# Gated units for two tiles in one slot, with products on 256 columns

## The chip, the cores and the metric

The kernel runs on one core of a Trainium2 chip, as one launch. The metric is the device time of that launch in microseconds. All values are float32.

## What is computed

The reference runs two layers of a trunk over a context of 128 tokens and a latent of 512 tokens, width 1024. Layer 0 is attention beside an RWKV mixer, layer 1 a convolution module, and each layer ends with an expert retrieval (`peer`). What matters here is layer 1's convolution module and the retrieval of both layers:

```python
def mixer_odd(h, w_pw1, b_pw1, w_dw, b_dw, ln_g, ln_b, w_pw2, b_pw2):
    u = h @ w_pw1 + b_pw1                               # 1024 -> 2048
    u = u[..., :D_CONV] * jax.nn.sigmoid(u[..., D_CONV:])
    u = depthwise_conv(u, w_dw) + b_dw                  # width 31
    u = jax.nn.silu(layernorm(u, ln_g, ln_b, LN_EPS))
    return u @ w_pw2 + b_pw2

def peer(h, w_q, keys, u_tab, v_tab):                   # per token: 8 heads, 16 experts each
    ...
        act = jax.nn.gelu(jnp.einsum('thkd,td->thk', u_tab[eidx], xb), approximate=False)
        wgt = (g * act.astype(jnp.float32)).astype(xb.dtype)
        return jnp.einsum('thk,thkd->td', wgt, v_tab[eidx])
```

Each token has 8 x 16 = 128 experts a layer, and an expert has a row of 1024 values in `u_tab` and one in `v_tab`.

## The kernel before

Up to some 900 us the kernel does layer 0's mixer. The rest, which the change touches, is `phase_trunk`. The 640 tokens are five tiles of 128: tile 0 is the context, tiles 1 to 4 the latent. Five tiles in two layers of `peer` make ten jobs, and a job has its own slot `s` of 128 rows (the loop over `PICKS`). In row `r` of slot `s`:

- GpSimd gathers, with an indirect DMA, one expert's `u` and `v` row for each of 128 tokens (128 x 2048 values) into one of `R = 8` places of `ring` (L1554). It waits until TensorE has used the place's earlier content (`used`).
- VectorE multiplies the `u` half with the tile's `h` and sums (`dot`, L1680), and does one step of choosing the experts of the next heads (`select`).
- ScalarE does, for two rows at a time, gelu, gate and the two scaled half identities `dg` (`weigh`, L1829 to L1840).
- TensorE adds the weighted `v` halves of two rows into PSUM with eight products on 512 columns (L2160 to L2164). I call these two rows a pair.

All other work of `phase_trunk` is laid beside these rows by hand. A generator such as `gated_units` yields the row number at which its next piece may be put, `Side` holds it, and `run_sides(sides, r)` writes out, on each engine, all pieces that are due by row `r` (TensorE and ScalarE look every second row). The row numbers thus set the order of instructions on an engine, not a time; semaphores do the rest. SyncE has no rows of its own: it goes through its pieces in the same order and stops at each wait.

Layer 1's convolution module of tile `i` has three parts, each with its slot:

- `GLU_SLOT(i)`, slots 2 to 6: the norm (`norm_one`: rows 12 to 21, scratch `y`, the two modulation rows in `pair`, and TensorE's transposes into `hT1`), then eight blocks of gated units, one each 4 rows from row 24. A block takes two weights of 128 x 1024 in `wg`, loaded by `for_glu` on SyncE's queue (L1500); TensorE does eight products each on the 128 columns of `hT1` (`units`, L2058), the second half two rows later; ScalarE does the sigmoid into `sg` (L1876), VectorE adds the bias, multiplies and writes `glu` (L1722). Each of the two `wg` places is loaded again once its product is done (`wg_used`).
- `CONV_SLOT(i)`, slots 2, 4, 5, 6, 7: the 31 taps from row 58 on. Five of eight blocks of channels are done on TensorE with scaled identities from ScalarE (`diagonals`, L1887; `taps`, L2076), three on VectorE. They need the units of the tile and of both neighbours, which is why tile 1's taps wait for tile 2's units.
- `POST_SLOT(i)`, slots 3, 5, 6, 7, 8: layer norm over channels (rows 4 to 18), the second linear layer (L2099, weights in `wq`, L1508), the gate and the sum (`mix`, rows 41 to 43), the second norm (`norm_two`, rows 46 to 50) and the queries and scores for the expert choice (L2126, weights in `wq`, L1480). `load_pair` (L1486, L1487) brings the two rows of 1024 values for each of norm, mix and second norm into the one `pair`, spread over all partitions (512 KB each); each load waits until the last user is done.

So slots 3, 5 and 6 hold units of one tile and the post part of another, slots 2 and 4 units alone, slots 7 and 8 the post part alone. On SyncE, `for_glu` and `for_post` write into one queue.

## Time and profile before

| | us |
|---|---|
| median of 3 runs | 4683.55 |
| lowest, highest | 4677.9, 4689.87 |
| the profiled execution | 4694.33 |
| its span, first to last instruction | 4692.5 |
| span's start to the end of slot 0 | 1408.6 |
| slots 1 to 9 | 3261.5 |
| TensorE, VectorE, ScalarE, GpSimd busy | 3236.1, 2775.4, 1728.1, 1468.9 |

The profile gives busy time for each engine; of the DMA it gives the share of time that the core's 16 DMA engines were busy (a little over 1 is possible, since packets overlap) and the GB/s that they moved. A slot is read as the time between two copies of `crossed` on ScalarE (L1848), which end a slot; the first of the ten starts at 1408.6 us, the last at 4670.1. "PEclk" is the granted clock of TensorE as a share of 2.4 GHz.

### The profile page before, as it was taken

To read this page: it belongs to the slowest core of one execution; us is meant where nothing else is said; L and a number is where in the kernel's file an instruction comes from. 1 tells how busy PE (TensorE), PEld (TensorE's weight loads), DVE (VectorE), ACT (ScalarE), POOL (GpSimd) and SP (SyncE) were. 2 spreads that over 40 slices of the span, in tenths; PEclk is the share of its full clock that TensorE was granted. 3 is DMA by queue.
4 is the path that set the end of the run, shared out by engine and by line. 5 is a ranking of instruction groups with operands and counts; after the bars stand their busy time and mean duration, and the time that the engine had idled before them with its cause. 6 is when DMAs were issued, how large, how long until landed. Compare 5 with 4: busy or idle time off the path is not lost. (4 is left out here: it accounts for less than half of the span.)

```text
span 4692.5 us, 72376 instructions
## 1 busy us (share of the span) xinstructions
PE 3236.1 (69%) x27071; PEld 1615.7 (34%) x27071; DVE 2775.4 (59%) x7104; ACT 1728.1 (37%) x5320; POOL 1468.9 (31%) x1298
## 2 busy tenths in 40 slices
PE   7988787777755556666665775786677677666555
PEld 4533676443211113323332332452344244223111
DVE  1257544335556766765656776585576776665764
ACT  1036222023222324544323553463454354332332
POOL 0000000012334443443334343343344443433443
PEclk9996898888877778988888887897898898888777
DMA  5161001268899999999999999999999999999998
GB/s 215 52 259 47 18 4 48 90 220 331 335 363 406 421 420 413 419 413 375 385 419 416 419 418 385 379 419 419 378 385 420 417 419 417 413 419 418 412 420 334
DMA packets 241982, 1567.70 MB, mean 334 GB/s; under 512 B 29942, under 2 KB 31057, under 8 KB 71265
## 3 DMA queue, kind: packets, MB, share of 16 engines
q0 software_dynamic: 184768, 1342.45, 69.8%
q1 hardware_dynamic: 56424, 220.51, 12.2%
q8 instruction: 216, 3.54, 0.3%
q14 instruction: 132, 1.08, 0.1%
q10 hardware_dynamic: 442, 0.12, 0.0%
HBM read 1559.88 MB, written 3.10 MB: 333 GB/s over the span
## 5 line engine op out<-in xcount | busy, mean ns | idle before, releaser
L1554 POOL DMA_INDIRECT t_ring<-in_peer_uv,t_eidx x1280 | 1461.4, 1142 | 3181.7 <-PE t_ps L2164 2051.3
L2160 PE MATMUL t_ps<-t_ring,t_dg 64*64 64x512 f32 x2560 | 1584.0, 751 | 1145.4 <-ACT t_dg L1840 1107.5
L1680 DVE SCALAR_TENSOR_TENSOR t_ring<-t_ring,t_hring 128x1024 f32<-128x1024 f32 x1024 | 1253.6, 1224 | 841.5 <-DMA t_ring<-in_peer_uv,t_eidx 810.3
L2164 PE MATMUL t_ps<-t_ring,t_dg 64*64 64x512 f32 x2560 | 1601.7, 758 | 0.0
L2163 PE MATMUL t_ps<-t_ring,t_dg 64*64 64x512 f32 x2560 | 1601.4, 758 | 0.0
L2161 PE MATMUL t_ps<-t_ring,t_dg 64*64 64x512 f32 x2560 | 1601.0, 758 | 0.0
L2160 PEld LDWEIGHTS t_ps<-t_ring,t_dg 64*64 64x64 f32 x2560 | 347.9, 157 | 2093.3 <-issue 2063.7
L1829 ACT ACTIVATE t_wgt<-t_dots 128x2 f32<-128x2 f32 x640 | 130.2, 203 | 1872.9 <-DVE t_ring L1680 1824.4
L1680 DVE SCALAR_TENSOR_TENSOR t_ring<-t_ring,t_early 128x1024 f32<-128x1024 f32 x256 | 313.8, 1226 | 313.8 <-DMA t_ring<-in_peer_uv,t_eidx 312.3
L1840 ACT ACTIVATE t_dg<-t_eye,t_wgt 128x64 f32<-128x64 f32 x1280 | 376.8, 340 | 2.7 <-ACT t_wgt L1834 1.9
L2164 PEld LDWEIGHTS t_ps<-t_ring,t_dg 64*64 64x64 f32 x2560 | 349.0, 157 | 0.0
L2163 PEld LDWEIGHTS t_ps<-t_ring,t_dg 64*64 64x64 f32 x2560 | 348.8, 157 | 0.0
L2161 PEld LDWEIGHTS t_ps<-t_ring,t_dg 64*64 64x64 f32 x2560 | 348.7, 157 | 0.0
L1834 ACT ACTIVATE t_wgt<-t_wgt,t_gate 128x1 f32<-128x1 f32 x1280 | 307.1, 287 | 26.1 <-ACT t_wgt L1829 0.4
L1887 ACT ACTIVATE t_early<-ident,vec 128x128 f32<-128x128 f32 x775 | 236.5, 389 | 0.7
L2058 PE MATMUL t_ps<-t_hT,t_wg 128*128 128x128 f32 x1280 | 180.6, 299 | 72.4 <-DMA t_wg<-in_cv_w_pw 72.4
L2076 PEld LDWEIGHTS t_ps<-t_early 128*128 128x128 f32 x1550 | 189.2, 195 | 74.7 <-ACT t_early L1887 43.2
L2058 PEld LDWEIGHTS t_ps<-t_hT,t_wg 128*128 128x128 f32 x1280 | 165.0, 209 | 144.6 <-issue 121.0
L2076 PE MATMUL t_ps<-t_early 128*128 128x128 f32 x1550 | 207.3, 287 | 5.4 <-PE t_ps L2126 0.5
L318 PE MATMUL fr_ps<-ev_hT,ev_wring 128*128 128x512 f32 x336 | 174.3, 601 | 0.0
L2126 PE MATMUL t_ps<-t_hT,t_wq 128*128 128x128 f32 x1280 | 162.3, 282 | 0.0
L2126 PEld LDWEIGHTS t_ps<-t_hT,t_wq 128*128 128x128 f32 x1280 | 156.4, 199 | 4.9 <-issue 4.9
(367 smaller groups left out, 4465.3 us busy)
## 6 DMA issues: line engine op xcount, KB each, us to landing
t_wq<-in_peer_w_q SPq DMA_DIRECT2D x112, 512.0 KB
ev_mod_ring<-in_mod_w SPq DMA_DIRECT2D x48, 1024.0 KB, 10.0
t_wg<-in_cv_w_pw SPq DMA_DIRECT2D x80, 512.0 KB
t_ring<-in_peer_uv,t_eidx POOLq DMA_INDIRECT x1280
t_wq<-in_cv_w_pw SPq DMA_DIRECT2D x40, 512.0 KB
t_pair<-modrows SPq DMA_DIRECT2D x25, 512.0 KB
ev_wring<-in_ab_w_in SPq DMA_DIRECT2D x21, 512.0 KB, 3.6
ev_qk<-in_ab_w_out SPq DMA_DIRECT2D x1, 4096.0 KB, 12.1
```

The source lines that it names most:

```text
L1554: pool.indirect_dma_start(ring[:, place[n], :], None, table, bass.IndirectOffsetOnAxis(ap=eidx[:, s % 2, r:r + 1], axis=0)).then_inc(row_i ...
L1680: V.scalar_tensor_tensor(ring[:, place[n], 0:D], ring[:, place[n], 0:D], 1.0, h_of(j), ALU.mult, ALU.mult, accum_out=dots[:, j % 2, r:r + ...
L1834: nc.scalar.activation(wgt[:, r + b:r + b + 1], wgt[:, r + b:r + b + 1], ACT.Copy, scale=gate[:, j % 2, r + b:r + b + 1]).then_inc(S["wgt_ ...
L1840: nc.scalar.activation(dg[:, n % DIAGS, :], eye[:], ACT.Copy, scale=wgt[:, r + b:r + b + 1]).then_inc(S["diag_set"], 1)
L1887: nc.scalar.activation(diag[:, n % BATCH, :], ident[:], ACT.Copy, scale=K.vec[:, col:col + 1]).then_inc(S["diag_ready"], 1)
L2058: last = nc.tensor.matmul(banks[:, 4 + b % 2, a * P:(a + 1) * P], wg[:, a, k, :], hT1[:, k, :], start=(k == 0), stop=(k == KD - 1))
L2076: nc.tensor.matmul(banks[:, 4 + b % 2, 0:P], diag[:, n % BATCH, :], glu[:, b, glu_col(i) + w:glu_col(i) + w + P], start=(w == 0), stop=(w ...
L2126: last = nc.tensor.matmul(banks[:, 6 + b % 2, 0:P], wq[:, n % 2, k, :], hT1[:, k, :], start=(k == 0), stop=(k == KD - 1))
L2160: nc.tensor.matmul(straight[low, cols], dg[low, n % DIAGS, :], ring[low, one, rows], **ends)
L2161: first = nc.tensor.matmul(straight[high, cols], dg[high, n % DIAGS, :], ring[high, one, rows], **ends)
L2163: nc.tensor.matmul(crossed[high, cols], dg[low, (n + 1) % DIAGS, :], ring[low, two, rows], **ends)
L2164: second = nc.tensor.matmul(crossed[low, cols], dg[high, (n + 1) % DIAGS, :], ring[high, two, rows], **ends)
```

## The change

The tiles' gated units are grouped: tiles 0 and 1 in slot 2, tiles 2 and 3 in slot 4, tile 4 alone in slot 6. In a group of two, both normed tiles are transposed (the first with rows from 4 on, the second from 12 on) into two halves of a buffer `both`, and each weight is used for one product on 256 columns. Such a block comes every 6 rows from row 22; tile 4's come every 4 rows, from row 22 as well. The sigmoid is one instruction for both tiles, with one buffer instead of two (ScalarE looks every second row, so `+ 3` and `+ 4` are the same place), and VectorE does two products of 128 columns in a block. Tile 3's norm uses the modulation rows that tile 2's has loaded. `CONV_SLOT` and `POST_SLOT` stay; in slots 2 and 4 taps and diagonals start at row 72, not 58. `cv`, `diag` and `hT1` get other places inside `early`, so that `both` can lie over `cv` and `hT1`.

```diff
-    GLU_SLOT = lambda i: i + 2
+    GROUPS = ((0, 1), (2, 3), (4,))
+    group = lambda i: i // 2
+    GLU_SLOT = lambda i: 2 + 2 * group(i)
...
+    glu_tick = lambda g, b: 22 + (6 if len(GROUPS[g]) == 2 else 4) * b
+    conv_tick = lambda i: 72 if CONV_SLOT(i) in (2, 4) else 58
+    glu_base = lambda i: 4 if i in (0, 2) else 12
...
+    units_in = lambda i: KD * (1 + (group(min(i + 1, NT - 1)) if i else 0))
...
-        early = sb("early", [P, 8672])
+        early = sb("early", [P, 9696])
...
-        cv = early[:, 5600:6624].rearrange("p (k c) -> p k c", k=KD)
+        cv = early[:, 7648:8672].rearrange("p (k c) -> p k c", k=KD)
+        both = early[:, 7648:9696].rearrange("p (t k c) -> p k t c", t=2, k=KD)
...
-        diag = early[:, 7648:7648 + BATCH * P].rearrange("p (n c) -> p n c", c=P)
-        hT1 = sb("hT1", [P, KD, P])
+        diag = early[:, 5600:5600 + BATCH * P].rearrange("p (n c) -> p n c", c=P)
+        hT1 = early[:, 8672:9696].rearrange("p (k c) -> p k c", k=KD)
...
-                def for_glu(i):
-                    yield 2
-                    load_pair(("norm", i), mod_row(i, 1), mod_row(i, 0))
+                def for_glu(g):
+                    for i in GROUPS[g]:
+                        yield glu_base(i) - 4
+                        if i != 3:
+                            load_pair(("norm", i), mod_row(i, 1), mod_row(i, 0))
                     for b in range(KD):
-                        yield 18 + 4 * b
+                        yield glu_tick(g, b) - 6
                         for a in range(2):
-                            n = 2 * (KD * i + b) + a
+                            n = 2 * (KD * g + b) + a
                             if n >= 2:
                                 sp.wait_ge(S["wg_used"], n - 1)
                             sp.dma_start(wg[:, a].rearrange("p k c -> p (k c)"), io["cv_w_pw1"][0, a * KD + b]).then_inc(wg_in[a], 16)
...
                 def norm_one(i):
-                    yield 14
+                    yield glu_base(i) + 2
                     mean(NORMS["norm", i])
-                    yield 16
+                    yield glu_base(i) + 4
                     invert(NORMS["norm", i])
                     dve.wait_ge(S["pair_in"], 32 * (PAIRS["norm", i] + 1))
+                    if i:
+                        dve.wait_ge(S["turned1"], i)
                     m = own(V.scalar_tensor_tensor(y, x[:, i, :], rstd[:, NORMS["norm", i]:NORMS["norm", i] + 1], pair[:, 0, :], ALU.mult, ALU.mult))
-                    yield 18
+                    yield glu_base(i) + 6
                     after_own(m)
                     V.tensor_tensor(y, y, pair[:, 1, :], ALU.add).then_inc(S["h1_done"], 1)
                     dve.wait_ge(S["h1_done"], i + 1)
-                    dve.sem_inc(S["pair_used"], 1)
-
...
-                def gated_units(i):
-                    col = glu_col(i) + PADC
+                    if i != 2:
+                        dve.sem_inc(S["pair_used"], 1)
+
+                def gated_units(g):
                     for b in range(KD):
-                        yield 24 + 4 * b + 6
-                        n = KD * i + b
+                        yield glu_tick(g, b) + 6
+                        n = KD * g + b
                         dve.wait_ge(S["sig_done"], n + 1)
                         bias = VEC["cv_b_pw1"] + b
-                        V.scalar_tensor_tensor(glu[:, b, col:col + P], banks[:, 4 + b % 2, 0:P], K.vec[:, bias:bias + 1], sg[:, b % 2, :],
-                                               ALU.add, ALU.mult).then_inc(S["glu_done"], 1)
+                        for e, i in enumerate(GROUPS[g]):
+                            col = glu_col(i) + PADC
+                            last = V.scalar_tensor_tensor(glu[:, b, col:col + P], banks[:, 4 + b % 2, e * P:(e + 1) * P], K.vec[:, bias:bias + 1], sg[:, e, :],
+                                                          ALU.add, ALU.mult)
+                        last.then_inc(S["glu_done"], 1)
...
-                    yield 61
+                    yield conv_tick(i) + 3
                     if i == 0:
                         dve.wait_ge(S["padded"], 4)
                     else:
                         dve.wait_ge(S["w_done"], i)
-                    dve.wait_ge(S["glu_done"], KD * min(i + 2 if i else 1, NT))
+                    dve.wait_ge(S["glu_done"], units_in(i))
...
                 def norm_one(i):
-                    yield 12
+                    yield glu_base(i)
                     act.wait_ge(S["summed"], GLU_SLOT(i))
-                    act.wait_ge(S["var_done"], done_by(POST_SLOT, GLU_SLOT(i)))
-                    square(y, i, NORMS["norm", i])
-                    yield 15
+                    act.wait_ge(S["q_done"], Q0 + NC * done_by(POST_SLOT, GLU_SLOT(i) - 1))
+                    dst = turned_tile(i)
+                    square(dst, i, NORMS["norm", i])
+                    yield glu_base(i) + 3
                     root(NORMS["norm", i])
-                    yield 21
+                    yield glu_base(i) + 9
                     act.wait_ge(S["turned1"], i + 1)
-                    act.wait_ge(S["q_done"], Q0 + NC * done_by(POST_SLOT, GLU_SLOT(i) - 1))
-                    nc.scalar.copy(hT1[:].rearrange("p k t -> p (k t)"), ps[:, 2, :]).then_inc(S["hTa_done"], 1)
-
-                def sigmoids(i):
+                    nc.scalar.copy(dst, ps[:, 2, :]).then_inc(S["hTa_done"], 1)
+
+                def sigmoids(g):
                     for b in range(KD):
-                        yield 24 + 4 * b + 3
-                        n = KD * i + b
+                        yield glu_tick(g, b) + 4
+                        n, members = KD * g + b, len(GROUPS[g])
                         act.wait_ge(S["g_done"], n + 1)
-                        if n >= 2:
-                            act.wait_ge(S["glu_done"], n - 1)
+                        if n:
+                            act.wait_ge(S["glu_done"], n)
                         bias = VEC["cv_b_pw1"] + KD + b
-                        nc.scalar.activation(sg[:, b % 2, :], banks[:, 4 + b % 2, P:2 * P], ACT.Sigmoid, bias=K.vec[:, bias:bias + 1]).then_inc(S["sig_done"], 1)
+                        nc.scalar.activation(sg[:, 0:members, :], banks[:, 4 + b % 2, 2 * P:(2 + members) * P].rearrange("p (t c) -> p t c", c=P),
+                                             ACT.Sigmoid, bias=K.vec[:, bias:bias + 1]).then_inc(S["sig_done"], 1)
...
                 def norm_one(i):
-                    yield 20
+                    yield glu_base(i) + 8
                     pe.wait_ge(S["h1_done"], i + 1)
                     if done_by(CONV_SLOT, GLU_SLOT(i) - 1):
                         pe.wait_ge(S["block_out"], NPE * done_by(CONV_SLOT, GLU_SLOT(i) - 1))
+                    if glu_base(i) > 4 and i < NT - 1:
+                        pe.wait_ge(S["hTa_done"], i)
                     for k in range(KD):
                         last = nc.tensor.transpose(ps[:, 2, k * P:(k + 1) * P], y[:, k * P:(k + 1) * P], ident[:])
                     last.then_inc(S["turned1"], 1)
 
-                def units(i):
+                def units(g):
+                    members = GROUPS[g]
+                    N = len(members) * P
                     for b in range(KD):
-                        yield 24 + 4 * b
-                        n = KD * i + b
+                        yield glu_tick(g, b)
+                        n = KD * g + b
                         if b == 0:
-                            pe.wait_ge(S["hTa_done"], i + 1)
+                            pe.wait_ge(S["hTa_done"], members[-1] + 1)
                         if n >= 2:
                             pe.wait_ge(S["glu_done"], n - 1)
                         for a in range(2):
                             if a:
-                                yield 26 + 4 * b
+                                yield glu_tick(g, b) + 2
                             pe.wait_ge(wg_in[a], 16 * (n + 1))
                             for k in range(KD):
-                                last = nc.tensor.matmul(banks[:, 4 + b % 2, a * P:(a + 1) * P], wg[:, a, k, :], hT1[:, k, :], start=(k == 0), stop=(k == KD - 1))
+                                rhs = both[:, k, :, :] if len(members) == 2 else hT1[:, k, :]
+                                last = nc.tensor.matmul(banks[:, 4 + b % 2, 2 * a * P:2 * a * P + N], wg[:, a, k, :], rhs, start=(k == 0), stop=(k == KD - 1))
```

The same shift of rows (`conv_tick(i)` for 58, `conv_tick(i) + 3` for 61) is made in `diagonals`, `blocks` and TensorE's `taps`. Lines of `phase_trunk` move by up to 27: L2058 is L2084 in the changed kernel, L2099 is L2125, L2160 is L2187, L1500 is L1513, L1508 is L1521, L1722 is L1739.

On SyncE, from the norm of slot 2 to the post part of slot 3. `t_pair` are modulation rows, `t_wg` the units' weights, `t_wq` from `in_cv_w_pw` the second linear layer's. Before:

```order
L1486 DMA t_pair<-modrows 128x1024
L1487 DMA t_pair<-modrows 128x1024
L1500 DMA t_wg<-in_cv_w_pw 128x1024 x16
L1486 DMA t_pair<-modrows 128x1024
L1487 DMA t_pair<-modrows 128x1024
L1508 DMA t_wq<-in_cv_w_pw 128x1024
L1500 DMA t_wg<-in_cv_w_pw 128x1024 x2
L1508 DMA t_wq<-in_cv_w_pw 128x1024 x2
L1486 DMA t_pair<-modrows 128x1024
L1487 DMA t_pair<-in_cv_b_pw 128x1024
L1500 DMA t_wg<-in_cv_w_pw 128x1024 x2
L1508 DMA t_wq<-in_cv_w_pw 128x1024 x2
```

and with the change:

```order
L1497 DMA t_pair<-modrows 128x1024
L1498 DMA t_pair<-modrows 128x1024
L1497 DMA t_pair<-modrows 128x1024
L1498 DMA t_pair<-modrows 128x1024
L1513 DMA t_wg<-in_cv_w_pw 128x1024 x16
L1521 DMA t_wq<-in_cv_w_pw 128x1024 x3
L1497 DMA t_pair<-modrows 128x1024
L1498 DMA t_pair<-in_cv_b_pw 128x1024
L1521 DMA t_wq<-in_cv_w_pw 128x1024 x5
L1497 DMA t_pair<-modrows 128x1024
L1498 DMA t_pair<-modrows 128x1024
L1491 DMA t_wq<-in_peer_w_q 128x1024 x16
```

Slot 3 has no `t_wg` any more, and slot 2 has two loads of rows ahead of its sixteen weights. On SyncE again, the start of slot 6. Before:

```order
L1486 DMA t_pair<-modrows 128x1024
L1487 DMA t_pair<-modrows 128x1024
L1521 DMA t_grow<-modrows 128x1024
L1508 DMA t_wq<-in_cv_w_pw 128x1024
L1500 DMA t_wg<-in_cv_w_pw 128x1024 x2
L1508 DMA t_wq<-in_cv_w_pw 128x1024 x2
L1486 DMA t_pair<-modrows 128x1024
L1487 DMA t_pair<-in_cv_b_pw 128x1024
L1500 DMA t_wg<-in_cv_w_pw 128x1024 x2
L1508 DMA t_wq<-in_cv_w_pw 128x1024 x2
L1500 DMA t_wg<-in_cv_w_pw 128x1024 x2
L1508 DMA t_wq<-in_cv_w_pw 128x1024 x2
```

and with the change:

```order
L1497 DMA t_pair<-modrows 128x1024
L1498 DMA t_pair<-modrows 128x1024
L1534 DMA t_grow<-modrows 128x1024
L1513 DMA t_wg<-in_cv_w_pw 128x1024 x2
L1521 DMA t_wq<-in_cv_w_pw 128x1024 x2
L1513 DMA t_wg<-in_cv_w_pw 128x1024 x2
L1521 DMA t_wq<-in_cv_w_pw 128x1024
L1497 DMA t_pair<-modrows 128x1024
L1498 DMA t_pair<-in_cv_b_pw 128x1024
L1521 DMA t_wq<-in_cv_w_pw 128x1024
L1513 DMA t_wg<-in_cv_w_pw 128x1024 x2
L1521 DMA t_wq<-in_cv_w_pw 128x1024 x2
```

The weights of units come two rows earlier against those of the post part: two `t_wg` blocks now stand ahead of the `t_pair` row from `in_cv_b_pw`. On TensorE, in slot 2, from the first half of a block of units to the second. Before:

```order
L2058 MATMUL t_ps<-t_hT,t_wg 128x128 x8
L2160 MATMUL t_ps<-t_ring,t_dg 64x512
L2161 MATMUL t_ps<-t_ring,t_dg 64x512
L2163 MATMUL t_ps<-t_ring,t_dg 64x512
L2164 MATMUL t_ps<-t_ring,t_dg 64x512
L2160 MATMUL t_ps<-t_ring,t_dg 64x512
L2161 MATMUL t_ps<-t_ring,t_dg 64x512
L2163 MATMUL t_ps<-t_ring,t_dg 64x512
L2164 MATMUL t_ps<-t_ring,t_dg 64x512
L2058 MATMUL t_ps<-t_hT,t_wg 128x128 x8
```

and with the change:

```order
L2084 MATMUL t_ps<-t_early,t_wg 128x256 x8
L2187 MATMUL t_ps<-t_ring,t_dg 64x512
L2188 MATMUL t_ps<-t_ring,t_dg 64x512
L2190 MATMUL t_ps<-t_ring,t_dg 64x512
L2191 MATMUL t_ps<-t_ring,t_dg 64x512
L2187 MATMUL t_ps<-t_ring,t_dg 64x512
L2188 MATMUL t_ps<-t_ring,t_dg 64x512
L2190 MATMUL t_ps<-t_ring,t_dg 64x512
L2191 MATMUL t_ps<-t_ring,t_dg 64x512
L2084 MATMUL t_ps<-t_early,t_wg 128x256 x8
```

Between the two halves of a block stands one pair, as before; each product has 256 columns. Behind the second half stood one pair up to the next block, now there are two.

## Rows read from the trace of the kernel before

**Rows 1.** The page: DMA by 40 equal slices of the span, and queue q0
```profile
DMA  5161001268899999999999999999999999999998
GB/s 215 52 259 47 18 4 48 90 220 331 335 363 406 421 420 413 419 413 375 385 419 416 419 418 385 379 419 419 378 385 420 417 419 417 413 419 418 412 420 334
...
q0 software_dynamic: 184768, 1342.45, 69.8%
```

**Rows 2.** Windows, one for each of slots 1 to 8; columns as printed
```profile
core 0: us, PE busy (x) PEld busy (x) DVE busy (x) ACT busy (x) POOL busy (x), PEclk, DMA share, GB/s
1408.60:1744.50 335.90, 190.86 (x1032) 49.51 (x1032) 221.12 (x572) 98.71 (x346) 149.28 (x132) 0.74 1.01 417
1744.50:2093.50 349.00, 231.71 (x1606) 115.64 (x1606) 247.56 (x679) 170.86 (x533) 145.11 (x128) 0.88 1.01 417
2093.50:2489.80 396.30, 253.90 (x1656) 127.46 (x1656) 230.64 (x589) 141.74 (x424) 147.86 (x128) 0.85 0.97 395
2489.80:2835.00 345.20, 231.63 (x1606) 113.71 (x1606) 248.40 (x679) 171.12 (x533) 144.87 (x128) 0.88 1.01 418
2835.00:3233.80 398.80, 286.60 (x1966) 159.09 (x1966) 255.28 (x685) 188.49 (x584) 147.98 (x128) 0.86 0.98 397
3233.80:3633.20 399.40, 281.30 (x1966) 156.91 (x1966) 254.13 (x685) 188.10 (x583) 152.46 (x128) 0.88 0.97 397
3633.20:3991.40 358.20, 253.99 (x1702) 125.43 (x1702) 251.50 (x672) 164.21 (x556) 148.92 (x128) 0.88 1.01 418
3991.40:4349.20 357.80, 221.14 (x1392) 90.09 (x1392) 230.52 (x585) 117.33 (x397) 141.07 (x128) 0.87 1.01 417
```

**Rows 3.** Waits (in total, times, longest): slot 2, slot 3's start, slot 6's start
```profile
POOL t_ring L1554 <- PE t_ps L2164: 183.1, 62, 6.9
...
POOL t_ring L1554 <- PE t_ps L2164: 126.0, 28, 20.7
...
DVE t_hring L1781 <- DMA t_pair<-modrows: 13.7, 1, 13.7
```

**Rows 4.** Windows, 40 us of slot 3
```profile
2260.00:2300.00 40.00, 24.89 (x172) 13.72 (x176) 29.45 (x77) 16.86 (x45) 15.73 (x12) 0.78 0.80 322
```

**Rows 5.** Timelines of SyncE, TensorE and VectorE in slot 3 (start, us, what, [idle before])
```profile
2164.80 2.77 SPq L1500 DMA_DIRECT2D t_wg<-in_cv_w_pw  x2
...
2183.84 3.75 PE L2058 MATMUL t_ps<-t_hT,t_wg 128*128 128x128 f32 x16 [12.50 <-DMA t_wg<-in_cv_w_pw]
...
2247.49 0.43 SPq L1486 DMA_DIRECT2D t_pair<-modrows  x1
...
2262.60 1.29 DVE L1781 SCALAR_TENSOR_TENSOR t_hring<-x,t_rstd,t_pair 128x1024 f32<-128x1024 f32 x1 [12.57 <-DMA t_pair<-modrows]
```

**Rows 6.** The page: DMA issues, with count and KB each
```profile
t_wg<-in_cv_w_pw SPq DMA_DIRECT2D x80, 512.0 KB
```

**Rows 7.** Timeline of TensorE in slot 3: a block of units, a product on 512 columns
```profile
2165.16 2.05 PE L2058 MATMUL t_ps<-t_hT,t_wg 128*128 128x128 f32 x16
...
2219.28 2.01 PE L2099 MATMUL t_ps<-t_wq,t_early 128*128 128x512 f32 x4
```

**Rows 8.** Timeline of TensorE: first and last instruction of two pairs of sixteen
```profile
2097.85 0.64 PE L2160 MATMUL t_ps<-t_ring,t_dg 64*64 64x512 f32 x1 [1.33 <-DVE t_early L1691]
...
2099.21 0.59 PE L2164 MATMUL t_ps<-t_ring,t_dg 64*64 64x512 f32 x1
...
2143.35 1.08 PE L2160 MATMUL t_ps<-t_ring,t_dg 64*64 64x512 f32 x1 [5.30 <-ACT t_dg L1840]
...
2145.98 1.06 PE L2164 MATMUL t_ps<-t_ring,t_dg 64*64 64x512 f32 x1
```

**Rows 9.** Windows: slot 2 up to 1860 us and behind it, 40 us of slot 5
```profile
1744.50:1860.00 115.50, 77.73 (x499) 36.67 (x500) 80.44 (x224) 49.32 (x132) 43.54 (x42) 0.82 1.01 413
1860.00:1940.00 80.00, 49.51 (x368) 28.39 (x366) 52.14 (x148) 40.56 (x114) 32.16 (x26) 0.94 1.02 418
2940.00:2980.00 40.00, 34.20 (x208) 18.83 (x206) 18.83 (x50) 14.91 (x35) 12.19 (x12) 0.91 0.98 393
```

**Rows 10.** Groups of ScalarE: table loads at the sigmoid's line (count, busy, mean ns)
```profile
L1876 ACT ACT_TABLE_LOAD x40 | 51.3, 1283 | 0.7
```

More of the change, by code:

```diff
@@ L1458, in phase_trunk @@
             for i in range(NT):
-                if GLU_SLOT(i) == s:
+                if GLU_SLOT(i) == s and i != 3:
                     PAIRS["norm", i] = len(PAIRS)
@@ L1465, in phase_trunk @@
         at_slot = lambda of, s: [i for i in range(NT) if of(i) == s]
+        groups_at = lambda s: [g for g in range(len(GROUPS)) if GLU_SLOT(GROUPS[g][0]) == s]
+        last_group = lambda s: sum(GLU_SLOT(members[0]) <= s for members in GROUPS)
+        PAIRS["norm", 3] = PAIRS["norm", 2]
         NORMS = {}
@@ L1537, in _ @@
                         sides.append(Side(next_keys()))
-                    sides += [Side(for_glu(i)) for i in at_slot(GLU_SLOT, s)]
+                    sides += [Side(for_glu(g)) for g in groups_at(s)]
                     sides += [Side(for_post(i)) for i in at_slot(POST_SLOT, s)]
@@ L1761, in mix @@
                     dve.wait_ge(S["pair_in"], 32 * (PAIRS["mix", i] + 1))
-                    if POST_SLOT(i) in [GLU_SLOT(k) for k in range(NT)]:
-                        dve.wait_ge(S["turned1"], POST_SLOT(i) - 1)
+                    if at_slot(GLU_SLOT, POST_SLOT(i)):
+                        dve.wait_ge(S["turned1"], done_by(GLU_SLOT, POST_SLOT(i)))
                     m = own(V.tensor_tensor(y, ps[:, 3, :], pair[:, 1, :], ALU.add))
@@ L1974, in _ @@
                     for i in at_slot(GLU_SLOT, s):
-                        sides += [Side(norm_one(i)), Side(sigmoids(i))]
+                        sides.append(Side(norm_one(i)))
+                    sides += [Side(sigmoids(g)) for g in groups_at(s)]
                     for i in at_slot(POST_SLOT, s):
@@ L2069, in taps @@
                         if m == 0:
-                            pe.wait_ge(S["glu_done"], KD * min(i + 2 if i else 1, NT))
+                            pe.wait_ge(S["glu_done"], units_in(i))
                             if i == 0:
@@ L2141, in _ @@
                     for i in at_slot(GLU_SLOT, s):
-                        sides += [Side(norm_one(i)), Side(units(i))]
+                        sides.append(Side(norm_one(i)))
+                    sides += [Side(units(g)) for g in groups_at(s)]
                     for i in at_slot(POST_SLOT, s):
```

16 lines of the change are left out of this document (9 added, 7 removed).

## The prediction

> **What bounds the kernel now.** I read the page's 40 slices first. From the 13th slice on (a slice is 117.3 us long, so from about 1408 us) the DMA digit is 9 and GB/s lies between 375 and 421, up to the last slice [rows 1]. No compute engine is near that: TensorE is busy for 69% of the span. In this part the kernel works through ten jobs, and each job fetches 128 times a block of 128 expert rows. That is 1280 gathers that carry 1342.45 MB, or 1.049 MB each [rows 1]. Per job, the windows [rows 2] show two kinds. Slots 2, 4, 7 and 8 run at 417 to 418 GB/s with a DMA share of 1.01; slots 3, 5 and 6 take 396.3, 398.8 and 399.4 us at 395 to 397 GB/s with a share of 0.97 to 0.98. So in the first kind the end is set by bytes, and in the second by bytes plus holes.
>
> The waits by window tell what the holes are. In slot 2, GpSimd (which issues gathers) never waits over 6.9 us for TensorE to free a ring place. In the first half of slot 3 it waits up to 20.7 us [rows 3], and the DMA share falls as low as 0.80 over 40 us [rows 4]. TensorE itself is held there: 12.50 us for a weight block of the gated units, which was issued at 2164.80, in SyncE's order right behind two `t_wq` blocks and two `t_pair` rows. VectorE waits 12.57 us for the `t_pair` rows issued at 2247.49 [rows 5]. Slots 3, 5 and 6 are those in which gated units (`for_glu`) and the second half of a convolution (`for_post`) share SyncE's one queue, where each load can stand behind another one's wait.
>
> **Bytes that go.** Each of eight blocks per tile loads two `t_wg` weights of 512 KB: 80 loads now [rows 6]. With three groups instead of five tiles there are 48. The `t_pair` rows of tile 3's norm go too (2 loads), since tile 2's are kept. That is 34 loads of 0.524 MB; at 417 GB/s [rows 2] one is 1.257 us of all engines, so 42.7 us in sum. The Trainium skill, "DMA: Bandwidth & Descriptors", section "Bandwidth", says that between HBM and SBUF the HBM side binds at about 358 GB/s for a core; by that the 34 loads would be an estimated 49.8 us. The trace does not agree: it has 417 to 418 GB/s over whole slots [rows 2].
>
> **Bytes and holes, slot by slot.** Instead of adding a price of holes to this, I take for each slot the slot of before that has the same work.
> - Slot 3 keeps the post part alone. So does slot 8 now: 357.8 us. 396.3 - 357.8 = 38.5 us less.
> - Slot 5 keeps post and taps, as slot 7 has now: 358.2 us, plus one `t_grow` load (1.3 us) that slot 7 lacks: 359.5. 398.8 - 359.5 = 39.3 us less.
> - Slot 2 gets the `t_pair` rows of tile 1 beside those of tile 0: 2 x 1.257 = 2.5 us more.
> - Slot 4 has 16 weight loads and one pair of rows before and after: 0.
> The sum is 38.5 + 39.3 - 2.5 = 75.3 us. Of this, 42.7 are bytes and the other 32.6 are holes and small traffic.
>
> **What the doubled products cost.** A block of 8 products on 128 columns (16 matmul instructions) took 2.05 us at the higher clock and 3.75 us where the clock was low [rows 5]; 4 instructions on 512 columns took 2.01 us, 0.50 each, so 256 columns are 0.25 each [rows 7]. Sixteen of those are 4.0 us, and twice the 128-column block is 4.1 us (7.5 at the low clock, by the 3.75 us block of [rows 5]). So grouping saves no TensorE time; it puts 31 us more (16 x 1.95) into slot 2 and into slot 4, off the path as long as TensorE keeps up. The order shows what it has to keep up with: in rows 22 to 70 of the slot, six picks a block. Gathers and loads need 6 x 2.51 + 2 x 1.257 = 17.6 us a block. TensorE needs three pairs, at 1.95 us (2097.85 to 2099.80) or 3.7 us (2143.35 to 2147.04) [rows 8], and two blocks of 4.1 or 7.5: 14.1 us at 2.4 GHz, 26.1 us at 1.2 GHz. The granted clock was 0.82 in the stretch with the units of slot 2, then 0.94 [rows 9]; at 0.95 the block is about 14.8 us, 84% of 17.6. The nearest row with as dense a TensorE is that of the 40 us from 2940: 34.20 us busy, 86%, with a DMA share of 0.98 where 1.01 is full [rows 9]. That is 3% lost. Over 8 x 17.6 = 141 us it is 4 us a slot, 8 us in both. The ends: 0 (the ring of 8 places takes it all), or what slot 3 lost. There 32.6 us of holes in two slots say 16 us for one, so 32 for two. I take 8, because the 12 to 13 us waits of slot 3 came from SyncE's queue, and in slots 2 and 4 that queue holds nothing but `t_wg` in these rows.
>
> **Slot 6** keeps gated units, post and taps together. The units start 2 rows earlier, and the order of SyncE's queue changes: the weights of the second block now stand ahead of the third `t_wq` and of the bias rows, which they followed before, and the last `t_pair` rows no longer wait for TensorE's row 46 but for its row 44. Two rows are 5 us of the 13.7 us that VectorE waited for such rows in slot 6 [rows 3]. I take 5 us off; the ends are 16 (its hole closes) and -3 (the sigmoid, now with one buffer, holds VectorE once a block for a little).
>
> **Taps 14 rows later.** In slots 2 and 4 taps run in rows 72 to 126, not 58 to 112. The same instructions at the same spacing; over the whole of slot 2 TensorE was busy for 231.71 of 349.0 us and VectorE for 247.56 [rows 2], so they stay hidden. The mean over channels at row 4 of the next slot reads what row 126 finishes: the cover shrinks from 20 rows to 6, 15 us. If it were gone, each of two slots would show one wait of a few us; I count 0, up to 5. On ScalarE each sigmoid costs a table load of 1.28 us and one back for Gelu [rows 10]; 16 fewer of each free 41 us there. It waits for VectorE most of the time, so that is worth 0. The second norm in slots 2 and 4 (two VectorE operations of 1.2 us, a copy of 1.0 on ScalarE, eight transposes) is hidden by the same slack: 0.
>
> **Waits that it adds.** VectorE's second norm (row 16) waits for TensorE's transposes of the first tile (row 12), and the dots of row 16 and on stand behind it; four rows, 10 us, cover it. On SyncE the second `t_pair` load of slot 2 waits for VectorE's row 10, with sixteen `t_wg` behind it; the first of these is needed at row 22, some 30 us on, and rows issued at 2247.49 had landed by 2262.60 [rows 5]. TensorE's second transposes (row 20) wait for ScalarE's copy (row 14), with the pair of rows 20 and 21 behind. The sigmoid of a block waits until VectorE has used the one before, with ScalarE's gelu behind it, and VectorE has two rows, 5 us, for that. Each is counted at 0; one that shows would cost at most a wait of 7 us as slot 2 has now on GpSimd's side [rows 3], and the ring of eight took those without a hole.
>
> **Sum.** -75.3 + 8 - 5 = -72.3 us. The profiled execution took 4694.33 us (span 4692.5), 10.8 us over the median of the runs, 4683.55; the difference is carried over to the median: 4683.55 - 72.3 = 4611 us.
>
> **The rivals.**
> 1. *The holes move.* TensorE's bursts hold the ring in slots 2 and 4 as slots 3 and 5 are held now: 16 us each in place of 4. For it: 84% is as dense as any stretch of now, and the single buffer for the sigmoid ties VectorE, ScalarE and TensorE once a block. Against: in rows 22 to 70 nothing else stands in SyncE's queue. Time: 4683.55 - 75.3 - 5 + 32 = 4635 us.
> 2. *No loss at all.* Slots 2 and 4 lose nothing, slot 6 closes: 4683.55 - 75.3 - 16 = 4592 us.
> 3. *Slower: TensorE bounds rows 22 to 70 at the low clock.* At 1.2 GHz a block needs 26.1 us against 17.6, 8.5 us more; 16 blocks are 136 us, and with the 75.3 and the 5 us gained 4739 us. It decides from 5.0 us a block on (80.3 / 16), so from a block of 22.6 us, a clock that stays low for most of it. Against: the clock rose as the stretch went on, from 0.82 to 0.94 [rows 9].
> 4. *It doesn't pay.* The slots without holes are set by something that counts gathers, not bytes, and the holes come back: within 14 us of 4684. Against: slot 1, nearly without loads, took 335.9 us, slots 7 and 8, with 28, took 358 [rows 2].
>
> **Chances.** Forecast (4597 to 4628) 0.68; rival 1 0.18; rival 2 0.06; rival 3 0.04; rival 4 0.04. The range must leave out no more than 0.2: from 4595 to 4642 it holds the forecast and nearly all of rival 1. A measurement of this kernel tells about 0.3%, 14 us, from no change. The forecast and rivals 1 and 2 are all faster by more than that: faster 0.92, same 0.04, slower 0.04.
>
> **What will show it.** Loads: `t_wg` x48 and 17.8 MB less in all. Slot 3 near 358 us and slot 5 near 360 at 417 GB/s, with no wait of GpSimd over 10 us: right; if they stay above 370, the holes were not of the shared queue. Slot 2 near 355 and slot 4 near 349: right; 365 and more is rival 1, above all with a DMA share under 0.95 in rows 22 to 70; a granted clock near 0.5 there is rival 3. Slot 6 near 394. The forecast would be wrong if the 256-column products were much dearer than 0.25 us an instruction.

## The result, and the profile after

| | us |
|---|---|
| changed kernel, median of 4 runs | 4598.51 (4595.88 to 4602.11) |
| kernel before, beside it | 4680.73 (4677.72 to 4689.87) |
| ratio, 95% interval | 0.9822 [0.9805, 0.9839] |
| its profiled execution, span | 4601.10, 4599.3 |

The change took 82 us off, 1.8%, where 72 were forecast. The time lies in the forecast range of 4597 to 4628, near its low end, 12.5 us under the 4611 forecast.

The windows of the changed kernel, slots 1 to 8, between two copies of `crossed` (L1867 there), with the columns of [rows 2]:

```profile
core 0: us, PE busy (x) PEld busy (x) DVE busy (x) ACT busy (x) POOL busy (x), PEclk, DMA share, GB/s
1405.00:1737.80 332.80, 188.62 (x1032) 49.28 (x1032) 220.72 (x572) 98.70 (x345) 146.32 (x132) 0.75 1.01 417
1737.80:2085.30 347.50, 251.68 (x1614) 130.65 (x1614) 250.32 (x686) 177.61 (x540) 145.11 (x128) 0.91 1.01 416
2085.30:2446.50 361.20, 231.75 (x1392) 96.90 (x1392) 228.84 (x582) 117.74 (x396) 142.71 (x128) 0.83 1.01 417
2446.50:2789.90 343.40, 251.99 (x1614) 131.02 (x1614) 253.15 (x691) 177.92 (x540) 144.14 (x128) 0.91 1.01 414
2789.90:3153.30 363.40, 254.50 (x1702) 125.86 (x1702) 251.76 (x675) 163.97 (x557) 152.48 (x128) 0.89 1.01 416
3153.30:3539.40 386.10, 280.46 (x1966) 157.22 (x1966) 253.70 (x682) 190.52 (x586) 143.34 (x128) 0.89 1.00 409
3539.40:3898.10 358.70, 257.67 (x1702) 126.88 (x1702) 251.33 (x672) 164.45 (x557) 143.54 (x128) 0.88 1.01 417
3898.10:4255.30 357.20, 220.80 (x1392) 91.05 (x1392) 229.80 (x585) 117.11 (x397) 140.90 (x128) 0.88 1.01 417
```

Against [rows 2], slots 3 and 5 have lost the share of 0.97 to 0.98 and stand at 1.01 with 361.2 and 363.4 us. Slots 2 and 4 carry twice the products (TensorE is busy for 20 us more in each, where 31 were forecast) at a full DMA share and a little less time. Slot 6 still has a hole, a smaller one. From these windows:

| slot | before | after | difference | forecast |
|---|---|---|---|---|
| 1 | 335.9 | 332.8 | -3.1 | 0 |
| 2 | 349.0 | 347.5 | -1.5 | +6.5 |
| 3 | 396.3 | 361.2 | -35.1 | -38.5 |
| 4 | 345.2 | 343.4 | -1.8 | +4 |
| 5 | 398.8 | 363.4 | -35.4 | -39.3 |
| 6 | 399.4 | 386.1 | -13.3 | -5 |
| 7 and 8 | 716.0 | 715.9 | -0.1 | 0 |

The list of DMA issues shows the loads that went, beside the 80 of [rows 6]; the last number is the median time from issue to landing:

```profile
t_wg<-in_cv_w_pw SPq DMA_DIRECT2D x48, 512.0 KB, 8.1
...
t_pair<-modrows SPq DMA_DIRECT2D x23, 512.0 KB, 11.6
...
t_pair<-in_cv_b_pw SPq DMA_DIRECT2D x5, 512.0 KB, 15.0
```

The packets sum up to 1549.80 MB against 1567.70 MB, 17.9 MB less. The waits of the changed kernel in the whole of slot 3 and in slot 6's first 207 us, in the form of [rows 3]:

```profile
POOL t_ring L1567 <- PE t_ps L2191: 198.7, 62, 6.4
...
POOL t_ring L1567 <- PE t_ps L2191: 128.1, 32, 16.1
...
PE t_ps L2084 <- DMA t_wg<-in_cv_w_pw: 16.8, 4, 11.3
...
DVE t_hring L1799 <- DMA t_pair<-modrows: 8.2, 1, 8.2
```

In slot 3 GpSimd now waits 6.4 us at most, where it was 20.7 [rows 3]. In slot 6, the one slot in which units and post part still meet, it is 16.1 us, and TensorE and VectorE wait for the same two kinds of load as before.

### The profile page after: what moved, and what is told of

Read it like the earlier page. It is cut to its first block and busy times, and to the rows that moved or that the text cites. A ratio compares the mean times of both kernels' runs of the same rounds, so it can differ in the third digit from the quotient of the medians.

```text
span 4599.3 us, 71228 instructions
## 1 busy us (share of the span) xinstructions
PE 3223.2 (70%) x26559; PEld 1588.6 (35%) x26559; DVE 2775.9 (60%) x7104; ACT 1695.2 (37%) x5282; POOL 1447.1 (31%) x1298
## 2 busy tenths in 40 slices
DMA packets 237081, 1549.80 MB, mean 337 GB/s; under 512 B 29398, under 2 KB 30513, under 8 KB 66369
## 5 line engine op out<-in xcount | busy, mean ns | idle before, releaser
L1567 POOL DMA_INDIRECT t_ring<-in_peer_uv,t_eidx x1280 | 1439.6, 1125 | 3110.3 <-PE t_ps L2191 1981.2
L2187 PE MATMUL t_ps<-t_ring,t_dg 64*64 64x512 f32 x2560 | 1578.4, 749 | 1124.7 <-ACT t_dg L1859 1102.5
L2187 PEld LDWEIGHTS t_ps<-t_ring,t_dg 64*64 64x64 f32 x2560 | 347.5, 156 | 2085.0 <-issue 2055.6
L2084 PE MATMUL t_ps<-t_early,t_wg 128*128 128x256 f32 (+1 forms) x768 | 157.0, 360 | 16.8 <-DMA t_wg<-in_cv_w_pw 16.8
L2152 PE MATMUL t_ps<-t_early,t_wq 128*128 128x128 f32 x1280 | 165.1, 285 | 0.0
L2152 PEld LDWEIGHTS t_ps<-t_early,t_wq 128*128 128x128 f32 x1280 | 159.6, 203 | 4.1 <-issue 4.1
L2084 PEld LDWEIGHTS t_ps<-t_early,t_wg 128*128 128x128 f32 x768 | 128.9, 198 | 74.6 <-issue 57.5
## 6 DMA issues: line engine op xcount, KB each, us to landing
t_ring<-in_peer_uv,t_eidx POOLq DMA_INDIRECT x1280, 13.3
```

Source lines behind the costliest of these rows:

```text
L1567: pool.indirect_dma_start(ring[:, place[n], :], None, table, bass.IndirectOffsetOnAxis(ap=eidx[:, s % 2, r:r + 1], axis=0)).then_inc(row_i ...
L2084: last = nc.tensor.matmul(banks[:, 4 + b % 2, 2 * a * P:2 * a * P + N], wg[:, a, k, :], rhs, start=(k == 0), stop=(k == KD - 1))
L2152: last = nc.tensor.matmul(banks[:, 6 + b % 2, 0:P], wq[:, n % 2, k, :], hT1[:, k, :], start=(k == 0), stop=(k == KD - 1))
L2187: nc.tensor.matmul(straight[low, cols], dg[low, n % DIAGS, :], ring[low, one, rows], **ends)
```

## The experiments

Two pictures of where the time came from had to be told apart. In mine, the end is set by bytes, and the holes (time in which less is moved than the 414 to 418 GB/s of a full slot) are waits behind other loads in SyncE's queue. In the other, the holes belong to the work itself (TensorE and VectorE in the rows where units and post part meet), or to any load beside it. Eleven runs follow; one of them is the changed kernel again, one a repeat. Ratios are against the kernel before, measured beside each, with 95% intervals; they and the medians can differ by some us in what they give, and where it matters both are told. Slot times are from one profile each: in six profiles with the same work in slots 3 and 5, slot 3 took 359.5 to 361.4 us and slot 5 361.8 to 364.9.

**Only the bytes put back.** In slots 3 and 5 of the changed kernel, where the weight places are idle, ScalarE makes 16 loads a slot into them that nobody uses:

```diff
+                def extra_loads(q):
+                    for b in range(KD):
+                        yield 24 + 6 * b
+                        if b == 0:
+                            act.wait_ge(S["wg_used"], 2 * KD * (q + 1))
+                        if b or q:
+                            act.wait_ge(S["extra_in"], 32 * (KD * q + b))
+                        for a in range(2):
+                            act.dma_start(wg[:, a]...).then_inc(S["extra_in"], 16)
...
+                            if b == 0 and a == 0 and g:
+                                sp.wait_ge(S["extra_in"], 32 * KD * g)
...
+                    if s in (3, 5):
+                        sides.append(Side(extra_loads((s - 3) // 2)))
```

The wait on SyncE holds the first real weight of slots 4 and 6 until the extra loads are in.

> The changed kernel with the 32 weight loads that the grouping removed put back as loads that nobody uses: 16 in slot 3 and 16 in slot 5, two every 6 rows, issued by ScalarE into the idle weight places, so not in SyncE's queue. Theory A (the end is set by bytes, and the holes came from the shared queue): slots 3 and 5 get 20 us longer each (361 to 381, 363 to 383), DMA share stays at 1.01, the whole is 40 us slower than the changed kernel (about 4639 us), still 42 us faster than before. Rival B (fewer, not smaller: the slots are set by a count of gathers): within 10 us of the changed kernel. Rival C (any 16 more loads beside the post part make the holes, whoever issues them): slots 3 and 5 return to 395 us or more, the whole to 4665 or more.

Measured: 4633.18 us, ratio 0.9897 [0.9877, 0.9917]. Slots 3 and 5 in its windows:

```profile
2088.60:2470.60 382.00, 236.40 (x1392) 96.62 (x1392) 229.83 (x584) 117.17 (x396) 142.91 (x128) 0.80 1.01 416
2812.00:3194.80 382.80, 261.20 (x1702) 127.14 (x1702) 251.59 (x673) 163.65 (x557) 143.56 (x128) 0.86 1.01 415
```

They are 20.8 and 19.4 us longer than in the changed kernel, 40.2 for 32 loads: 1.26 us a load, where 1.257 was worked out. With a scatter of one to three us a slot, the agreement to the last digit is chance. The whole is 35 us slower than the changed kernel, by the medians and by the ratios, or 1.1 us a load; 40 had been expected. The profiled execution was the slowest of four. The share stays at 1.01. So bytes are paid in full or nearly so, and 16 more loads beside the post part make no hole when they come from elsewhere.

What did the holes cost? The same two slots of the kernel before took 396.3 and 398.8 us [rows 2], 14.3 and 16.0 more than here. But slot 3 of before moved fewer bytes (395 GB/s in 396.3 us are 156.5 MB, against 158.9 here). Taken by the rate, 395 and 397 GB/s in place of 416, an estimated 20 and 18 us of those slots were hole. Between the two readings lie 30 to 38 us for both slots.

**Only the modulation rows moved, in the kernel before.**

```diff
-                        if k == 2:
-                            load_pair(("mix", i), mod_row(i, 2), io["cv_b_pw2"][0])
                     yield 43
-                    load_pair(("keys", i), mod_row(i, 4), mod_row(i, 3))
...
+                def pairs_of_post(i):
+                    row = lambda kind: K.modrows[stream(i), (6 + kind) * D:(7 + kind) * D]
+                    for tick, key, first, second in ((20, "mix", row(2), io["cv_b_pw2"][0]), (44, "keys", row(4), row(3))):
+                        yield tick
+                        act.wait_ge(S["pair_used"], PAIRS[key, i])
+                        act.dma_start(pair[:, 0, :], first.partition_broadcast(P)).then_inc(S["pair_in"], 16)
+                        act.dma_start(pair[:, 1, :], second.partition_broadcast(P)).then_inc(S["pair_in"], 16)
```

> The kernel before, with only one thing moved: the modulation rows of mix and of the second norm (the pair loads of the post part, 512 KB each) are issued by ScalarE at rows 20 and 44, not by SyncE between the weight loads. Theory A (holes of slots 3, 5 and 6 come from loads that stand behind another load's wait in the one queue): VectorE's wait of 12 to 14 us for these rows falls to 8 us or less in each, and TensorE's of 12.5 us for the second block's weight falls too; slots 3, 5, 6 get 5 to 12 us shorter each, the whole 15 to 35 us faster than before. Rival B (the holes come from the work of TensorE and VectorE in those rows, not from the queue): within 8 us of before.

Measured: 4644.22 us, ratio 0.9929 [0.9910, 0.9949]: 39 us by the medians, 33 by the ratio, at the upper end of what was expected or a little over it. The windows of slots 3, 5 and 6, and the waits in slot 3's first 210 us:

```profile
2080.20:2464.80 384.60, 257.38 (x1656) 127.00 (x1656) 231.53 (x593) 141.57 (x423) 143.77 (x128) 0.86 1.00 407
2809.00:3196.70 387.70, 285.65 (x1966) 157.31 (x1966) 256.13 (x689) 188.26 (x583) 146.22 (x128) 0.89 1.00 411
3196.70:3584.50 387.80, 289.09 (x1966) 160.65 (x1966) 255.26 (x687) 188.37 (x584) 146.03 (x128) 0.88 1.00 409
```

```profile
POOL t_ring L1551 <- PE t_ps L2169: 124.9, 33, 10.4
...
PE t_ps L2063 <- DMA t_wg<-in_cv_w_pw: 17.7, 7, 5.1
...
DVE t_hring L1778 <- DMA t_pair<-modrows: 1.4, 1, 1.4
```

Every slot with both kinds of work is 11 to 12 us shorter, with the same loads and products (slot 3 moved 156.5 MB in both, by its rates). TensorE's longest wait for a weight is 5.1 us where it was 12.50, VectorE's for the rows 1.4 for 12.57, GpSimd's longest 10.4 for 20.7. The two pictures part here: the work was left as it was, so it can't be the cause of the part that went; where and when the loads are issued is. The edit changes the issuing engine and the row of issue together, and no run parts these two. Nor is the hole gone. The three slots run at 407 to 411 GB/s, not 416, which makes an estimated 5 to 8 us of hole that is left in each, of some 18 to 20 before; TensorE's waits for weights in these 210 us still sum up to 17.7.

**Only the row of the units moved, in the kernel before.** All five tiles' units two rows earlier, as tile 4's are in the change:

```diff
-                        yield 18 + 4 * b
+                        yield 16 + 4 * b
...
-                        yield 24 + 4 * b
+                        yield 22 + 4 * b
```

(and the same two rows for the second half, the sigmoid and VectorE's product).

> The kernel before with one part of the change alone: all five tiles' blocks of units start at row 22 in place of 24, loads of their weights two rows earlier too; no grouping. Theory A (order and rows close most of the hole that units and post part make together): slots 3, 5 and 6 each get about 13 us shorter, the whole 35 to 40 us faster than before (about 4643 us), with no byte less. Rival B: no slot moves by over 4 us, the whole within 10 us of before.

Measured: 4661.59 us, ratio 0.9963 [0.9951, 0.9975]: 17 us by the ratio, 21 by the medians. Slots 3, 5 and 6:

```profile
2081.60:2470.10 388.50, 249.37 (x1656) 123.51 (x1656) 232.04 (x592) 144.22 (x425) 139.46 (x128) 0.87 0.99 403
2814.90:3207.30 392.40, 280.67 (x1966) 156.49 (x1966) 253.61 (x685) 190.96 (x586) 140.52 (x128) 0.89 0.99 403
3207.30:3600.70 393.40, 287.82 (x1966) 158.06 (x1966) 256.22 (x686) 191.13 (x586) 148.20 (x128) 0.87 1.00 406
```

That is 7.8, 6.4 and 6.0 us a slot, half of the 13 I had expected after seeing slot 6 of the changed kernel. The gain is there, at half the size.

**The same row, undone in the changed kernel.** Tile 4's units from row 24:

```diff
-    glu_tick = lambda g, b: 22 + (6 if len(GROUPS[g]) == 2 else 4) * b
+    glu_tick = lambda g, b: 22 + 6 * b if len(GROUPS[g]) == 2 else 24 + 4 * b
```

> The changed kernel with one part undone: tile 4's blocks of units start at row 24 again, not at row 22 (slot 6), so that SyncE's order in slot 6 is that of the kernel before. Theory A (slot 6 became 13.3 us shorter, 399.4 to 386.1, because the weights and modulation rows are asked for in another order and two rows earlier): slot 6 returns to 396 to 400 us and the whole is 10 to 14 us slower than the changed kernel (4609 to 4612 us). Rival B (it came from the single sigmoid buffer, the place of hT1, or chance): slot 6 stays at 384 to 388, the whole within 4 us of 4598.5.

Measured: 4602.94 us, ratio 0.9844 [0.9822, 0.9867]; slot 6 at 395.6. The slot came near to what theory A said; the whole is 4 us above the 4598.5 of the changed kernel, not 10 to 14. Slot 6 was also at 388.5, 390.1 and 393.2 us in three other kernels with the changed kernel's instructions in that slot, so one profile says little, and both kernels were measured again side by side.

> The changed kernel as it is, on the same chip and in the same rounds as the next one, which puts tile 4's units back to row 24: its slot 6 was 386.1 us in one profile, but 388.5, 390.1 and 393.2 in three kernels with the same instructions in that slot. Expected: 390 +- 4 us for slot 6, 4598 us for the whole.

> The changed kernel with tile 4's units at row 24. Theory A (order and rows are worth 6 us in slot 6, as in three slots of the kernel before): slot 6 at 395 to 397, the whole 4 to 8 us slower than the changed kernel of the same call. Rival B (they are worth nothing, and slot 6 only scatters): within 2 us of it.

Measured: 4595.13 us, ratio 0.9806 [0.9792, 0.9821], and 4600.94 us, ratio 0.9821 [0.9804, 0.9838]: 5.8 us between the medians, though the intervals overlap. Slot 6 of the one and of the other, and what VectorE waits for the modulation rows in each:

```profile
3141.50:3534.10 392.60, 285.47 (x1966) 158.69 (x1966) 256.50 (x686) 191.23 (x585) 146.39 (x128) 0.87 1.00 406
...
DVE t_hring L1799 <- DMA t_pair<-modrows: 9.1, 1, 9.1
```

```profile
3145.70:3540.60 394.90, 286.38 (x1966) 158.57 (x1966) 255.37 (x685) 188.26 (x583) 149.03 (x128) 0.87 0.98 401
...
DVE t_hring L1799 <- DMA t_pair<-modrows: 12.2, 1, 12.2
```

With the units at row 22 VectorE waits 8.2 and 9.1 us in two profiles, at row 24 13.2 and 12.2: with the gain goes this wait, 3 to 5 us shorter. Five profiles with row 22 have slot 6 at 386.1, 388.5, 390.1, 392.6 and 393.2 us, 390.1 in the mean; two with row 24 at 395.6 and 394.9; the kernel before, and before with later taps (below), at 399.4 and 398.5. So the row is worth about 5 us in slot 6. Some 4 us lie between 395 and 399; with two profiles on either side they may be something else in the change, the single sigmoid buffer or the new places in `early`, or scatter. No run tells which.

**Both small moves, in the kernel before.** Units at row 22 and the modulation rows from ScalarE (the two edits above).

> The kernel before with both small moves: units of all tiles at row 22, and the modulation rows of the post part issued by ScalarE; no grouping, no byte less. Theory A (the holes of slots 3, 5 and 6 are the waits behind other loads in SyncE's queue, and both moves take away some of the same): slots 3, 5, 6 at 382 to 385 us, which is what the same bytes took when they came from elsewhere, the whole 42 to 48 us faster than before (4635 to 4640 us); what is left to the changed kernel is the 42 us of bytes. Rival B (the moves add up, 17 and 39): 56 us faster.

Measured: 4645.02 us, ratio 0.9912 [0.9894, 0.9930]: 41 us by the ratio, 42 by the medians. By the ratios alone a sum of 17 and 33 us can't be told from this, since each of these has an interval of 11 to 18 us. The slots can tell. Slots 3, 5 and 6:

```profile
2078.40:2462.10 383.70, 262.76 (x1656) 129.03 (x1656) 232.51 (x592) 144.45 (x425) 143.81 (x128) 0.84 1.00 408
2805.50:3195.40 389.90, 285.33 (x1966) 158.09 (x1966) 257.30 (x689) 191.63 (x585) 150.80 (x128) 0.89 1.00 409
3195.40:3581.50 386.10, 287.64 (x1966) 159.88 (x1966) 255.61 (x686) 191.47 (x586) 150.28 (x128) 0.88 1.01 412
```

In sum they are 0.4 us shorter than with the modulation rows alone, where adding up would have made them 20 us shorter. So the moves take away the same hole; they don't add up. About half of the gain of the changed kernel is thus to be had without grouping anything.

**The width of the product.** The changed kernel with two runs of eight products on 128 columns for each weight:

```diff
-                            for k in range(KD):
-                                rhs = both[:, k, :, :] if len(members) == 2 else hT1[:, k, :]
...
+                            for e in range(len(members)):
+                                for k in range(KD):
+                                    rhs = both[:, k, e, :] if len(members) == 2 else hT1[:, k, :]
...
```

(each product then writes its own 128 columns).

> The changed kernel, but in slots 2 and 4 each weight is used for two runs of eight products on 128 columns in place of one run of eight on 256; loads, rows and groups stay. Theory A (the gain is that each weight is loaded once for two tiles; the width of the product is nothing, since TensorE has slack): 32 instructions of 0.128 us are 4.1 us for what took 3.72, slots 2 and 4 within 3 us of 347.5 and 343.4, the whole within 10 us of 4598.5. Rival B (256 columns are what keeps slots 2 and 4 full): each 8 us or more longer.

Measured: 4595.91 us, ratio 0.9816 [0.9796, 0.9835]. The blocks on TensorE, of this kernel and then of the changed one:

```profile
1813.59 3.84 PE L2085 MATMUL t_ps<-t_early,t_wg 128*128 128x128 f32 x32
```

```profile
1813.10 3.72 PE L2084 MATMUL t_ps<-t_early,t_wg 128*128 128x256 f32 x16
```

Slots 2 and 4 took 348.6 and 341.1 us. The width is worth nothing here; the weight that is loaded once is the gain.

**TensorE's slack.** Each run of eight products on 256 columns done twice:

```diff
-                            for k in range(KD):
+                            for k in [k for _ in members for k in range(KD)]:
```

> The changed kernel, but in slots 2 and 4 each run of eight products on 256 columns is done twice (7.4 us for 3.72), loads and rows as they are. A block of six rows has 17.6 us by bytes; TensorE then needs 3 x 1.95 + 4 x 3.72 = 20.7 us. Theory A (the block is set by the dearer of the two, and the slack now is 17.6 less 13.3 us): slots 2 and 4 get about 3 to 5 us a block longer, 25 to 40 us each, the whole 4648 to 4678 us. Rival B (the ring takes more, since other rows have slack): under 10 us each.

Measured: 4651.26 us, ratio 0.9932 [0.9912, 0.9952]. Rows 22 and on of slot 2, from 1820 us, first in this kernel and then in the changed one:

```profile
1820.00:1860.00 40.00, 37.30 (x213) 25.06 (x213) 19.15 (x52) 13.85 (x32) 13.52 (x12) 1.00 0.91 352
1860.00:1900.00 40.00, 37.35 (x210) 26.19 (x212) 19.81 (x56) 13.36 (x37) 11.34 (x11) 1.00 0.93 356
```

```profile
1820.00:1860.00 40.00, 31.38 (x180) 18.54 (x182) 25.23 (x70) 18.53 (x46) 16.27 (x14) 0.96 1.01 419
1860.00:1900.00 40.00, 30.45 (x176) 16.68 (x168) 25.72 (x75) 18.01 (x44) 15.85 (x14) 0.91 1.02 419
```

Slots 2 and 4 are 374.9 and 370.9 us long, 27.4 and 27.5 more than in the changed kernel, 3.4 a block for the 3.1 that the sum gave. A block then needs more TensorE time (20.7 us) than its bytes take (17.6), TensorE is busy for 93% and the DMA share falls to 0.91. In the changed kernel TensorE is busy for 73 to 82% of each 40 us in the rows of the units (the windows above and those that follow, in both slots), at 1.01 to 1.02, and costs nothing.

**The taps alone, and a faster version.** The kernel before with the taps of slots 2 and 4 at row 72, and the changed kernel with the modulation rows from ScalarE. The edits are those shown in the change and above.

> The kernel before with one part of the change alone: taps, diagonals and blocks of slots 2 and 4 start 14 rows later (72), nothing grouped. Theory A: hidden, slots 2 to 5 within 3 us each, the whole within 10 us of before. Rival B (with the cover from row 126 to row 4 of the next slot gone, the post part of slots 3 and 5 starts late): 5 us or more on slots 3 and 5 each.

Measured: 4681.89 us, ratio 1.0000 [0.9987, 1.0013]. Slots 2 to 5 took 347.2, 395.1, 341.6 and 400.1 us. Slot 6 took 398.5. The shift is free, and the six rows that are left as cover are enough.

> The changed kernel with the modulation rows of the post part issued by ScalarE at rows 20 and 44, not by SyncE. Theory A (only slot 6 has two users of SyncE's queue left): slot 6 from 386 to about 380, slots 3, 5, 7, 8 within 3 us, the whole 4 to 8 us faster than the changed kernel (about 4592 us) and the fastest so far. Rival B: the wait for the rows was part of every post slot: 3 us or more off each of five slots, the whole 15 us or more.

Measured: 4595.63 us, ratio 0.9814 [0.9798, 0.9831]. Slot 6:

```profile
3148.40:3534.30 385.90, 291.35 (x1966) 159.17 (x1966) 257.07 (x688) 191.58 (x586) 152.52 (x128) 0.87 1.01 413
```

Its share is 1.01 and its rate 413 GB/s, so its hole is nearly closed; still its time is that of the changed kernel's first profile (386.1), 4 us under the mean of five, and not the 380 expected. Slots 3 and 5 stay at 361.2 and 361.9. The whole is 2.9 us below the changed kernel of the first measurement and 0.5 us above that of the later one, so these runs don't show it to be faster. None is clearly faster than the changed kernel.

## Why the prediction came out as it did

- **Bytes** (42.7 us for 34 loads at 1.257): right. The same loads from elsewhere cost 40.2 us for 32 by the slots, 35 by the whole. The figure of about 358 GB/s that the prediction cites from the Trainium skill, "DMA: Bandwidth & Descriptors", section "Bandwidth", and by which the bytes would have been an estimated 49.8 us, does not hold in this kernel: slots 2 to 5 of the changed kernel run at 414 to 417 GB/s too.
- **Bytes and holes of slots 1 to 5** (-75.3 without the cost of doubled products): measured -76.9. The single slots were off by 2 to 4 us each. Slots 8 and 7 as models for 3 and 5 missed that SyncE runs ahead and asks for loads of the next slot (in the changed kernel it issues four for slot 4 from 2388.40 us on), so slots 3 and 5 gained 35.1 and 35.4 in place of 38.5 and 39.3; slots 1, 2 and 4 gained what these lacked. The mechanism is borne out by two runs: one changes only where and when the modulation rows are issued, the other puts only the bytes back.
- **Doubled products** (+8 us, 4 a slot): mis-sized; slots 2 and 4 show no cost. The failing step was to read the 3% that the row at 2940 us lacks [rows 9] as the price of a TensorE that is 86% busy, without looking for denser rows. The same slot of the kernel before, some 130 us later, has one at a full share. And with the modulation rows moved to ScalarE, the same stretch (105 to 145 us into slot 5) is full as well, with TensorE at 80%. First that row of before, then that of the run:

```profile
3075.00:3115.00 40.00, 36.75 (x296) 24.66 (x287) 32.47 (x99) 26.46 (x95) 15.91 (x15) 0.96 1.01 419
```

```profile
2914.00:2954.00 40.00, 31.87 (x208) 18.02 (x208) 22.65 (x60) 14.79 (x35) 12.79 (x11) 0.96 1.02 414
```

So the trace of before already had TensorE at 92% with nothing lost, and "84% is as dense as any stretch of now", said for rival 1, was misread. The TensorE time that is added was mis-sized too: a run of eight products on 256 columns took 3.72 us, not 4.0, and a slot got 20 us, not 31.
- **Slot 6** (-5 us): the row order was worth about 5 us, as worked out, and a shorter wait for the modulation rows goes with it. The profile showed 13.3, five profiles 9 in the mean; some 4 us are open, and the rest of the 13.3 is scatter of that slot.
- **The taps** and the added waits at 0: right, the taps by a run of their own. VectorE's and ScalarE's added waits put no hole into slots 2 and 4; their share is 1.01.
- **The rivals.** "No loss at all" (4592) lies nearer to the measured 4598.5 than the forecast of 4611 does, since it had both terms at their low ends: true for slots 2 and 4, half true for slot 6. "The holes move" fell with the share of slots 2 and 4. "Slower" needed a low clock, and the granted clock of those rows was 0.85 to 0.96. Its break-even of 22.6 us a block fits the run with the products done twice: that adds 3.4 us a block and 53 us in all; the 82 us of gain would by this estimate be used up at 5.1 us a block, or 22.7. "It doesn't pay" fell with the bytes put back: 16 loads more made a slot some 20 us longer with no gather more.

How far off was it? The slots of the two profiles differ by 89.6 us where 72.3 were forecast. Of these 17.3 us, 8 are the doubled products, 8.3 slot 6, and 1.0 all the other slots together. By the medians the gain is 82.2, so 7 us of the 17 are how executions differ, and part of slot 6's 8.3 is among them. The miss against 4611 is some 3 us larger than that in the gain, since the kernel before ran at 4680.73 beside the changed one and not at 4683.55. The forecast was near for its reasons: the two terms that were off, 8 and 4 to 8 us, are small beside the 75 that held.

## What to carry to other kernels

Where DMA bounds a stage, read its share slot by slot: bytes and holes are two bills, and a hole can be a load that stands in one engine's queue behind another load's wait. To size the part that is holes, put the bytes back from an idle queue, or move one small load to another queue; the four 512 KB loads of modulation and bias rows in each post slot, moved, were worth 33 to 39 us here, nearly all of it in slots 3, 5 and 6. How busy an engine is does not say what it costs: TensorE at 92% lost nothing in one stretch, at 93% it lost a tenth of the DMA share in another, where its work for a block was longer than the block's bytes. So compare the time that the engine needs with the time that the bytes need, look through the whole trace for denser stretches before you price one, and find the limit by doing the work twice.

## What the runs showed of the hardware

- Two short moves of loads (rows to ScalarE, units two rows earlier) saved 33 and 17 us alone and 41 together by the ratios; in slots 3, 5 and 6 they saved 34.4 and 20.2 us alone and 34.8 together, so they shortened the same holes.
- Sixteen instructions on 256 columns took 3.72 us and thirty-two on 128 took 3.84, both where the granted clock was 0.96 to 1.0: the wide form saves 3%. Twice the 2.05 us of [rows 7], which the forecast took, is 4.10, more than one unbroken run of thirty-two.
- Slot 6 scattered by 7 us between five profiles of the same instructions; in the same five slot 7 scattered by 4.3 and slot 8 by 3.2. Slot 0, with the phases ahead of it, scattered by 14 us over all profiles (1394.3 to 1408.6).
